# Two attention heads at a time: scores on the row halves of the array, values on its column halves

## The reference

```python
# layer 1, MLA: 8 heads, 96 wide (64 + 32 rotary, the 32 shared by all heads), values 64 wide, causal
s = jnp.einsum('bqhd,bkhd->bhqk', qb, k) * scale
p = masked_softmax(s, key_pos[None, :] <= q_pos[:, None])
o = jnp.einsum('bhqk,bkhd->bqhd', p, v)
# layer 2, NSA: 16 heads of 64, 4 key groups; three branches, mixed by gates of their own
out = gb[..., 0:1] * o_c + gb[..., 1:2] * o_s + gb[..., 2:3] * o_w
# layers 3 and 4: 4 neighbourhood heads (with a bias), 6 dilated heads (with a log weight), 6 heads on 2 key heads
mix = jnp.concatenate([rms_norm_2(out_a, og[:NA_W]), rms_norm_2(out_d, ...), rms_norm_2(out_c, ...)], axis=-1)
```

## Time and profile before

| | |
|---|---|
| median of 3 runs | 1872.05 us (1867.49 to 1873.01) |
| span of the profiled execution | 1863.5 us (first to last instruction; its own time isn't recorded beside it) |
| TensorE busy, matmul | 1771.7 us, 95% |
| VectorE busy | 1028.1 us, 55% |
| ScalarE busy | 850.3 us, 46% |
| MLA attention, 302.0 to 320.3 | 18.3 us, TensorE busy 17.2, mean granted clock 1.00 |
| NSA, from its query transposes to its attention, 794.9 to 841.3 | 46.4 us, TensorE busy 36.6, clock 0.85 |
| NSA attention, 842.0 to 931.2 | 89.2 us, TensorE busy 89.2, VectorE 47.0, ScalarE 43.6, clock 0.96 |
| first later layer, 1230 to 1277 | 47.0 us, TensorE busy 45.9, VectorE 26.3, clock 0.93 |
| second later layer, 1585.8 to 1630 | 44.2 us, TensorE busy 43.2, clock 1.00 |

### The profile page before, as it was taken

How to read it: one execution, slowest core, us unless ns; L and a number is a source line. 1 busy time by engine, 2 the same in 40 slices (tenths; PEclk the granted TensorE clock), 3 DMA queues, 4 the chain that set the end, 5 groups by cost and what they waited for, 6 DMA issues and landing times.

```text
span 1863.5 us, 29052 instructions
## 1 busy us (share of the span) xinstructions
PE 1771.7 (95%) x11809; PEld 1575.7 (85%) x11809; DVE 1028.1 (55%) x1306; ACT 850.3 (46%) x1187; POOL 148.4 (8%) x190
## 2 busy tenths in 40 slices
PE   7999998999999999989999998989999998989998
PEld 7999885899989998975689997955899988579997
DVE  6444555544454455655555445665655567565554
ACT  5344455444344334334444334554544454555443
POOL 0000001000000000410000002440000027000000
PEclk9999998999999999989999999989999999999999
DMA  7555431555545554420045555610455565015552
GB/s 263 190 188 180 160 134 46 194 190 180 180 162 189 190 181 145 150 91 23 1 143 185 180 181 133 216 59 7 171 184 176 184 181 181 1 52 199 201 180 91
DMA packets 40548, 276.87 MB, mean 149 GB/s; under 512 B 5505, under 2 KB 6290, under 8 KB 7570
## 3 DMA queue, kind: packets, MB, share of 16 engines
q1 hardware_dynamic: 39010, 271.00, 41.4%
q0 software_dynamic: 1456, 4.72, 1.6%
HBM read 274.65 MB, written 1.05 MB: 148 GB/s over the span
## 4 chain that ended last, share of the span: by engine, by line
PE 87%; DVE 4%; ACT 4%; POOL 3%; issue 1%; DMA 0%; SPq 0%; POOLq 0%; DVEq 0%; ACTq 0%
PE bank L639 19%; PE bank L620 14%; PE bank L622 14%; PE bank L621 14%; PE bank L600 4%; PE bank L693 4%; PE bank L551 3%; PE bank L552 3%; PE bank L553 3%; PE bank L734 2%; PE bank L708 2%; POOL proj L478 1%; DVE w_lo L1306 1%; ACT work L1028 1%; ACT w_hi L1018 1%
## 5 line engine op out<-in xcount | busy, mean ns | idle before, releaser
L1306 DVE TENSOR_TENSOR w_lo<-raw,w_hi 128x2048 fp32r<-128x2048 f32 x255 | 587.8, 2309 | 531.8 <-ACT w_hi L1018 530.9
L1018 ACT ACTIVATE w_hi<-raw 128x2048 fp32r<-128x2048 f32 x255 | 487.2, 1917 | 561.0 <-PE bank L622 400.3
L620 PE MATMUL bank<-xt_hi,w_hi 128*128 128x256 f32 x2112 | 600.1, 284 | 5.3 <-DVE xt_lo L1338 5.3
L621 PE MATMUL bank<-xt_lo,w_hi 128*128 128x256 f32 x2112 | 598.2, 283 | 0.0
L622 PE MATMUL bank<-xt_hi,w_lo 128*128 128x256 f32 x2112 | 598.2, 283 | 0.0
L620 PEld LDWEIGHTS bank<-xt_hi,w_hi 128*128 128x128 f32 x2112 | 405.7, 192 | 9.2 <-issue 5.0
L621 PEld LDWEIGHTS bank<-xt_lo,w_hi 128*128 128x128 f32 x2112 | 406.0, 192 | 2.5
L622 PEld LDWEIGHTS bank<-xt_hi,w_lo 128*128 128x128 f32 x2112 | 405.8, 192 | 0.0
L639 PE MATMUL bank<-w_hi,h_hi 128*128 128x512 f32 x528 | 208.3, 394 | 0.2
L639 PE MATMUL bank<-w_hi,h_lo 128*128 128x512 f32 x528 | 208.5, 395 | 0.0
L639 PE MATMUL bank<-w_lo,h_hi 128*128 128x512 f32 x528 | 208.2, 394 | 0.0
(11 more groups left out here) (297 smaller groups left out, 1806.6 us busy)
## 6 DMA issues: line engine op xcount, KB each, us to landing
raw<-in_stream SPq DMA_DIRECT2D x255, 1024.0 KB, 4.9
work<-in_rpb POOLq DMA_DIRECT2D x32, 64.0 KB, 3.7
X<-in_x SPq DMA_DIRECT2D x2, 512.0 KB, 4.1
prob<-in_cmp_w POOLq DMA_DIRECT2D x1, 1024.0 KB, 5.2
O<-in_cmp_w POOLq DMA_DIRECT2D x1, 1024.0 KB, 6.9
out<-X SPq DMA_DIRECT2D x1, 1024.0 KB, 4.0
cst<-in_consts SPq DMA_DIRECT2D x1, 776.0 KB, 6.0
O<-in_final_gain POOLq DMA_DIRECT2D x1, 512.0 KB, 4.3
```

What stands on the lines that cost most here:

```text
L620: pe.matmul(o, w_hi[:, sl, cols], xt_hi[:, k, :], start=(k == 0), stop=False)
L621: pe.matmul(o, w_hi[:, sl, cols], xt_lo[:, k, :], start=False, stop=False)
L1018: act.activation(w_hi[:, sl, :], raw[:, sl, :], ACT.Copy).then_inc(hi_done, 1)
L1306: dve.tensor_tensor(w_lo[:, sl, :], raw[:, sl, :], w_hi[:, sl, :].bitcast(F32), ALU.subtract).then_inc(lo_done, 1)
```

## The change

Jobs are taken in duos, two heads at a time.

- Queries and keys of two heads are transposed together, 128 columns at a time, so that head one lies in partitions 0 to 63 and head two in 64 to 127. The groups become 6 for NSA (4 and 2) and 7 for each later layer. Keys that several heads share are written to both halves: four copies per group in NSA, five in the last group of the later layers (three on ScalarE, then two on VectorE).
- scores(m) issues the matmuls of both heads in turn, each on its half of the array's rows. MLA's heads have 96 rows and use the array as before. The mask becomes one matmul of 256 columns per job.
- values(m) issues the matmuls of both heads in turn, each on its half of the array's columns.
- The compressed scores alternate row halves and banks, with one wait of TensorE for itself in the middle.
- There are four score banks and two for the transposed probabilities, which move from prob to KT; prob holds four jobs. The later layers have one output bank where there were two.
- TensorE's order becomes scores(m+1), turn_p(m), values(m-1), and VectorE's as below.

```diff
-S_BANKS = (0, 1, 6)
+S_BANKS = (0, 1, 6, 7)
+T_BANKS = (2, 3)
...
+                def scores(m):
...
+                    duo = [(jobs[i], bank[S_BANKS[i % 4]]) for i in (2 * m, 2 * m + 1)]
                     for qt in range(NT):
-                        n = ncols(job, qt)
-                        plain = not job["causal"] and job["bias"] is None
-                        ins = pe.matmul(dst[:, qt * S:qt * S + n], qT[0:job["d"], job["q"], qt * P:(qt + 1) * P],
-                                        kT[0:job["d"], job["k"], 0:n], start=True, stop=plain)
+                        for job, dst in duo:
+                            n = ncols(job, qt)
+                            r = job["rows"]
+                            plain = not job["causal"] and job["bias"] is None
+                            ins = pe.matmul(dst[:, qt * S:qt * S + n], qk[r, job["q"], qt * P:(qt + 1) * P],
+                                            qk[r, job["k"], 0:n], start=plain or qt == 0, stop=plain)
+                            if qt == 1 and plain:
+                                ins.then_inc(s_done, 1)
+                    for job, dst in duo:
                         if job["causal"]:
...
+                            both = dst[:, :].rearrange("p (b n) -> p b n", n=P)[:, 0:4:3, :]
+                            pe.matmul(both, ident_b[:, :], causal_b[:, :].unsqueeze(1).to_broadcast([P, 2, P]),
+                                      start=False, stop=True).then_inc(s_done, 1)
...
+                def turn_p(m):
+                    for i in (2 * m, 2 * m + 1):
+                        pe.wait_ge(p_scaled, j0 + i + 1)
+                        if m:
+                            pe.wait_ge(pt_evac, j0 + i - 1)
...
+                    if br == 0 and pair >= 1 and stage[:3] == "sec":
+                        pe.wait_ge(o_copied, 8 * int(stage[3]) + pair)
...
+                    pe.wait_ge(pt_evac, j0 + 2 * m + 2)
+                    for kt in range(2):
+                        for i in (2 * m, 2 * m + 1):
+                            job = jobs[i]
+                            dst = ob[(LOW, HIGH)[i % 2], 0:S]
...
                 scores(0)
-                scores(1)
-                for i in range(len(jobs)):
-                    scores(i + 2)
-                    turn_p(i)
-                    values(i - 1)
...
-                values(len(jobs) - 1)
+                for m in range(n_duos(stage)):
+                    scores(m + 1)
+                    turn_p(m)
+                    values(m - 1)
+                    if stage[:3] == "sec" and m >= 3:
+                        square_sums(m - 3)
+                values(n_duos(stage) - 1)
...
                     for t in range(NT):
                         for h in range(NS_H):
...
-                                            qT[0:64, h, t * P:(t + 1) * P], kcT_[0:64, g * 32:(g + 1) * 32],
+                            g, j, e = h // 4, h % 4, h % 2
+                            r, tt = (LOW, HIGH)[e], (t + e) % 2
+                            ins = pe.matmul(bank[6 + tt][:, (j * 4 + g) * 32:(j * 4 + g + 1) * 32],
+                                            qk[r, h // 2, tt * P:(tt + 1) * P], kcT[r, g * 32:(g + 1) * 32],
                                             start=True, stop=True)
-                    ins.then_inc(c_s, 1)
+                        ins.then_inc(c_s, 1)
+                        if t == 0:
+                            pe.wait_ge(c_s, 1)
...
+                for m in range(n_duos(stage) + 2):
+                    if m < n_duos(stage):
+                        exponentials(2 * m)
+                        exponentials(2 * m + 1)
+                    if 1 <= m <= n_duos(stage):
+                        evac(2 * m - 2)
+                        evac(2 * m - 1)
+                    pair_out(stage, pair_done(stage, m - 2))
...
                 maxima(0)
                 maxima(1)
-                scale(0)
-                for i in range(len(jobs)):
-                    maxima(i + 2)
-                    scale(i + 1)
-                    lo_part(pair_after(stage, i, 2))
...
+                for m in range(n_duos(stage)):
+                    maxima(2 * m + 2)
+                    maxima(2 * m + 3)
+                    scale(2 * m)
+                    scale(2 * m + 1)
+                    lo_part(pair_done(stage, m - 2))
```

More of the change, by code:

```diff
@@ L341, in sec_job @@
                         v=lambda kt: proj[:, kt, VC + g * 64:VC + g * 64 + 64])
-        heads["sec0"] = heads["sec1"] = [sec_job(2 * (7 - i // 2) + i % 2) for i in range(16)]
+        heads["sec0"] = heads["sec1"] = [sec_job(7 - i, e) for i in range(8) for e in range(2)]
         JOBS_PER_PAIR = {"mla": 2, "nsa": 4, "sec0": 2, "sec1": 2}
[L347 to L351, removed]
@@ L353, in late_pairs, with pair_done, n_duos @@
-        def late_pairs(stage, lag):
-            n, jobs = JOBS_PER_PAIR[stage], len(heads[stage])
-            return [q for q in range(jobs // n) if (q + 1) * n - 1 + lag >= jobs]
+        def pair_done(stage, m):
+            n = JOBS_PER_PAIR[stage] // 2
+            return m // n if m >= 0 and m % n == n - 1 else None
+        def n_duos(stage):
+            return len(heads[stage]) // 2
         o_t = O[:, :, :].rearrange("p t (a s) -> p (t a) s", s=S)
@@ L376, in ft_groups @@
                 return gs
[L377 to L385, removed]
@@ L397, in ft_scale @@
         def ft_scale(stage, g):
-            return 0.125 if stage == "nsa" and g < NS_H // 2 else 1.0
+            return 0.125 if stage == "nsa" and g < NS_H // 4 else 1.0
         def ncols(job, qt):
@@ L701, in scores @@
[L701 to L710, removed]
@@ L712, in values @@
-                def values(i):
-                    if i < 0:
-                        return
[L716 to L736, removed]
-                    else:
-                        ins = pe.matmul(dst, job["v"](1), pts_of(i % 2, S, 2 * S), start=False, stop=last)
-                    ins.then_inc(pv_done, 1)
@@ L1209, in pair_out @@
                 act.wait_ge(pv_done, JOB0[stage] + (pair + 1) * JOBS_PER_PAIR[stage])
-                src = bank[4 + pair % 2][:, 0:S]
+                src = bank[4 if stage[:3] == "sec" else 4 + pair % 2][:, 0:S]
                 if stage[:3] != "sec":
@@ L1444, in maxima @@
                     dve.wait_ge(s_done, j0 + i + 1)
-                    b, job = bank[S_BANKS[i % 3]], jobs[i]
+                    b, job = bank[S_BANKS[i % 4]], jobs[i]
                     if "dil" in job:
```

251 lines of the change are left out of this document (153 added, 98 removed).

## The result

The changed kernel takes 1905.78 us as the median of four runs (1901.44 to 1908.26), beside 1870.03 us (1867.49 to 1873.01) for the kernel before: 1.0194 times as long, 95% interval 1.0171 to 1.0217, so it is slower, by just under 2%. I had forecast 1915 us, slower, with 1864 to 1950 as the range. The profiled span went from 1863.5 to 1906.5 us, +43.0, more than the 35.8 between the medians: the execution profiled before was a short one (its span lies 6.5 under the median; the other runs' spans lie about 2 under their times), the one profiled after was the longest of the four (1908.26).

A forecast was written before the change was run, and what follows sets the result against it. TensorE was taken to bound the kernel, with 87% of the chain of waits. -5 us at the full clock and +48 for the clock gave +43, with 8.6 between span and median left: 1915 us, range 1864 to 1950.

The forecast's parts named there:

- The order: Attention loop: lookahead lost, TensorE waits 1.9 us after each NSA duo's scores for VectorE's scaled probabilities; ScalarE not late.
- The sum at the full clock: Whole kernel, clock never falling: -14 - 2 + 3 + 8 = -5 us.
- ahead of NSA: Transposes, compressed scores and key copies before the NSA attention: together -14 us.
- NSA attention: 16 duos at the full clock, 5.35 us each against 5.42, the last without a stall: -2 us.
- MLA: Four duos of unpaired heads at the full clock, 5.5 us against 4.30 per pair: +3 us.
- later layers: The two later attention stages at the full clock: about +4 us per layer, +8 in all.
- The halves: NSA duo: scores on row halves 1.13 us instead of 2.54; values on column halves 1.0, what one job did.
- rival 3: Values: column halves don't overlap; +33 - 5, 1900 us at high clock, 1930 to 1940 at low; chance 0.08.
- rival 4: Scores: row halves gain nothing for 256 columns; +42 - 5, 1909 us at the full clock; chance 0.04.
- The clock: Attention: stalls halve TensorE's clock; +121 us if all low, share taken as 0.4, so +48.
- 1: Attention: the clock holds despite the waits; -5 us, 1867, not slower; chance 0.22.
- 2: Attention: the clock stays low throughout; +121 - 5, 1988 us, or 1950 for most of it; chance 0.08.

The follow-up runs named there:

- e1: The changed kernel with VectorE's two scalings of a duo moved ahead of the next duo's two maxima; 1795.0 us.
- e2: The changed kernel with TensorE alone reordered, its scores issued two duos ahead, VectorE's order kept; 1788.0 us.
- e3: The changed kernel with dead matmuls filling TensorE's wait ahead of the transposes (4, 8 or 5 per duo); 1862.9 us.
- e11: e2 with the transposes of the duo's second job issued between the two jobs' values; 1819.3 us.
- e10: e2 with scores issued job by job and the first job's mask or bias between the two jobs' scores; 1814.5 us.
- e12: e2 with scores, transposes and values issued job by job, so neither half finds its partner; 1842.6 us.
- e9: The changed kernel with about half of e3's dead matmuls in its stalls (2, 4 or 3 per duo); 1863.4 us.
- e4: The kernel before, without pairs, with only VectorE's one-step lookahead taken away (scale(i) for scale(i+1)); 2085.8 us, one run.
- e5: e2 with the scores of a duo issued job by job instead of in turn, all else kept; 1791.0 us.

## Why the prediction was right

**The order.** Right as put. The stall after the scores was 1.91 us for 1.9 reckoned, released by VectorE's scaled P; exponentials were done before VectorE came to them; ScalarE was not late. e1 and e2 show the cause by two independent edits.

**The sum at the full clock** (-5) can be read off e3: -7.6 us between the medians, -2.4 between the profiled spans (1863.5 and 1861.1), for the reason given under the result. Term by term, on the spans: ahead of NSA -16.5 (forecast -14); NSA attention -1.2 (-2), duo 5.44 (5.35), of which some 3 us are the clock's, by an estimate from the mean clocks there (0.96 before, 1.00 in e3); MLA +3.8 (+3); later layers +1.9 and +5.0 inside the attention and +1.8 each ahead of it (+4 each in all). Those 1.8 are the ready keys, which I had at 0.4: TensorE waits 2.66 us for them where it waited 0.87, because the program makes VectorE's two copies wait for ScalarE's three (L1491), as VectorE's row in the changed kernel shows:

```profile
1248.76 1.13 DVE L1493 COPY QT<-bank 64x512 f32<-64x512 f32 x2 [1.51 <-ACT QT L1162]
```

Both read one PSUM bank; copies from separate banks were not tried.

**The halves.** A duo's scores with masks took 1.08 us (forecast 1.13) and its values 0.81, or 1.24 with the compressed ones, mean 1.03 (1.0), both at the full clock in e3. Compressed scores: 64 records in 4.0 us (4.4). The value that had no row, a pair for the price of one, was taken rightly; e11 excludes rival 3. Against rival 4 (no gain for 256 columns) there is a row of the changed kernel itself, eight records of 256 columns in the time in which the earlier trace rows have four:

```profile
1257.20 1.13 PE L718 MATMUL bank<-QT 64*128 64x256 f32 x8
```

e10 and e12 agree. The rule of the Trainium skill that I cited (TensorEngine Tiling (Array Packing), Theoretical Speedup) allows up to 2x; the runs agree: 0.86 us for two jobs' values, 0.79 for one's.

**The clock** (+48) was right in sum, 43 us between the medians of the changed kernel and e3, and wrong in its parts. With the share of 0.4, NSA should have lost 16 us, MLA 4 and each later layer 14; against e3 they lost 22.4, 6.3 and 6.8, and some 3 more fell on stretches behind the attention, 1.0 of them where the product after MLA began at the low clock (23.0 us at a mean clock of 0.96, for 22.0 before). Held against my prices for the low clock throughout (41, 10 and 35), these are shares of 0.55, 0.63 and 0.19: the errors cancelled, and that was luck. So what was wrong inside the right sum is one share of 0.4 for all three kinds of attention. I had also not seen that the two levels could alternate within one duo: in most NSA duos the clock was 1.00 over the wait and 0.50 over the values and a varying part of the transposes and scores around them, so the one shown took 6.76 us. The price of a duo that is low throughout was near: 7.77 measured (with compressed values), for a mean of 7.9.

**The total.** Forecast +43, between the medians +35.8. The two parts measured -7.6 and +43. That the spans differ by 43.0, just as forecast, is luck: the short execution profiled before and the long one after make up 7 us of it. The 1915 us came out 9 too high: 7 by the smaller change of the medians, 2 because the median before is 1870.03 by four runs where I had 1872.05 by three.

**Rivals.** 1 (clock holds, 1867) is what e3 and e9 give: 1863. 2 did not come in the changed kernel, but nearly so in e4 (0.54). 3 and 4 fell.

## What to carry to other kernels

When a software pipeline is regrouped, write down for each in-order engine which step of which group stands in front of the one that the critical engine waits for; the lookahead was worth 111 to 118 us here, more than the halves (up to 55). An experiment that fills a stall with dead work tells the cost of the wait from the cost of the clock. And a loop that waits on one engine should be priced once more with its dense part at the low clock: in this one much of that part ran at 0.50 in nearly every NSA duo.

## What the runs showed of the hardware

- Matmuls on different row halves ran side by side in both orders of issue that were tried, unless one that takes the whole array stood between them: 0.86 us for two jobs' scores in e2, 0.87 in e5, 0.86 each in e10. The same goes for column halves: 0.86 us for two jobs' values in e2, 0.79 each in e11.
- A TensorE without a gap can stay at the low clock. In e10, from 830 to 856, it was busy all the time at 0.50, and was back at 1.00 by 858; what kept it low and what ended it stay open.

```profile
830.00:840.00 10.00, 10.00 (x36) 6.14 (x36) 6.23 (x24) 2.98 (x12) 0.00 (x0) 0.50 0.08 34
...
858.00:868.00 10.00, 10.00 (x72) 6.50 (x70) 7.83 (x29) 6.00 (x24) 0.00 (x0) 1.00 0.01 2
```

- Two dead matmuls in a wait of 1.9 us were enough to hold the clock (e9, 0.98 in NSA), although 0.95 us of waiting was left in every duo:

```profile
854.54 0.55 PE L739 MATMUL bank<-cst,prob 128*128 128x128 f32 x3 [0.95 <-DVE prob L1544]
```
